# One operation for two expert blocks: silu, multiplication and the copies of the transposed activations in an expert SwiGLU stage

## What is computed

```python
def swiglu(h, wg, wu, wd):
    return (jax.nn.silu(h @ wg) * (h @ wu)) @ wd

def moe_swiglu(h, router, eg, eu, ed):
    ...
    top_v, top_i = lax.top_k(logits, TOP_K)
    ...
    for e in range(N_EXPERTS):
        out = out + combine[:, e:e + 1] * swiglu(t, eg[e], eu[e], ed[e])
```

## Time and profile before

| | |
|---|---|
| median of 3 runs | 1416.88 us (1416.75 to 1418.26) |
| span of the profiled execution | 1415.5 us |
| expert stage in it | from about 450 us to 1403 us |
| PE busy | 1397.5 us, 99% of the span |
| DVE busy | 1147.9 us, 81% |
| ACT busy | 945.4 us, 67% |
| chain that ended last | PE 96%, DVE 3%, ACT 1% |

### The profile page before, as it was taken

The page is one execution under the profiler, slowest core; times in us unless marked ns, Lnnn a source line. Parts: engine busy times, 40 slices in busy tenths (PEclk is TensorE's granted clock), DMA queues, the critical chain, the costliest instruction groups (busy, mean ns, idle before and its releaser), DMA issues.

```text
span 1415.5 us, 18473 instructions
## 1 busy us (share of the span) xinstructions
PE 1397.5 (99%) x6936; PEld 1160.4 (82%) x6937; DVE 1147.9 (81%) x1061; ACT 945.4 (67%) x880; POOL 85.3 (6%) x65
## 2 busy tenths in 40 slices
PE   8999999999999999999999999999999999999997
PEld 6898888887988888888888888888888888888885
DVE  5766645566576989988998998988899899898997
ACT  4645444345646777777777777777777777777775
POOL 2140000001132000000000000000000000000200
PEclk9999999999999999999999999999999999999998
DMA  9434555552444999999999999999999999999992
GB/s 351 162 120 181 208 181 200 183 208 91 148 164 179 361 386 364 387 386 368 383 390 373 375 392 385 361 374 393 370 382 390 373 380 388 389 356 376 421 387 116
DMA packets 63184, 438.20 MB, mean 310 GB/s; under 512 B 7199, under 2 KB 7377, under 8 KB 11906
## 3 DMA queue, kind: packets, MB, share of 16 engines
q1 hardware_dynamic: 58896, 423.20, 78.1%
q0 software_dynamic: 4064, 13.84, 2.5%
q10 hardware_dynamic: 146, 0.07, 0.0%
HBM read 430.79 MB, written 6.29 MB: 309 GB/s over the span
## 4 chain that ended last, share of the span: by engine, by line
PE 96%; DVE 3%; ACT 1%; issue 0%; DMA 0%; DVEq 0%; ACTq 0%
PE ps L1828 50%; PE ps L1852 26%; PE ps L1516 4%; PE ps L1531 3%; PE ps L1619 3%; PE ps L1844 2%; PE ps L1493 2%; PE ps L1888 1%; DVE w_lo L332 1%; PE ps L1608 1%; PE ps L1553 0%; PE ps L1977 0%; PE ps L1563 0%; ACT w_hi L327 0%; PE ps L1474 0%
## 5 line engine op out<-in xcount | busy, mean ns | idle before, releaser
L332 DVE TENSOR_TENSOR w_lo<-raw,w_hi 128x2048 fp32r<-128x2048 f32 x397 | 913.8, 2304 | 173.7 <-ACT w_hi L327 172.0
L327 ACT ACTIVATE w_hi<-raw 128x2048 fp32r<-128x2048 f32 x399 | 764.0, 1915 | 211.6 <-PE ps L1852 109.1
L1828 PE MATMUL ps<-w_hi,xT_hi 128*128 128x512 f32 x1040 | 411.1, 395 | 0.5 <-DVE xT_lo L1196 0.5
L1828 PE MATMUL ps<-w_lo,xT_hi 128*128 128x512 f32 x1040 | 405.5, 390 | 0.0
L1828 PE MATMUL ps<-w_hi,xT_lo 128*128 128x512 f32 x1040 | 404.8, 389 | 0.0
L1828 PEld LDWEIGHTS ps<-w_lo,xT_hi 128*128 128x128 f32 x1040 | 195.2, 188 | 41.6
L1828 PEld LDWEIGHTS ps<-w_hi,xT_hi 128*128 128x128 f32 x1040 | 195.4, 188 | 39.8 <-DVE xT_lo L1196 0.7
L1828 PEld LDWEIGHTS ps<-w_hi,xT_lo 128*128 128x128 f32 x1040 | 195.5, 188 | 38.8
L1852 PE MATMUL ps<-w_hi,aT_hi 128*128 128x512 f32 x524 | 205.9, 393 | 0.0
L1852 PE MATMUL ps<-w_lo,aT_hi 128*128 128x512 f32 x524 | 204.4, 390 | 0.0
L1852 PE MATMUL ps<-w_hi,aT_lo 128*128 128x512 f32 x524 | 204.0, 389 | 0.0
(11 more groups left out here) (307 smaller groups left out, 1112.6 us busy)
## 6 DMA issues: line engine op xcount, KB each, us to landing
raw<-in_stream SPq DMA_DIRECT2D x400, 1024.0 KB, 7.2
outs<-work POOLq DMA_DIRECT2D x7, 512.0 KB, 9.1
gain<-in_gains POOLq DMA_DIRECT2D x4, 512.0 KB, 5.3
h<-in_x SPq DMA_DIRECT2D x2, 512.0 KB, 6.6
raw<-in_stream SPq DMA_DIRECT2D x2, 512.0 KB, 6.1
tokens<-big POOLq DMA_DIRECT2D x2, 512.0 KB, 3.8
out<-work SPq DMA_DIRECT2D x4, 256.0 KB, 2.6
cst<-in_consts SPq DMA_DIRECT2D x1, 581.0 KB, 12.2
```

The costliest lines, as they stand in the source:

```text
L327: nc.scalar.activation(home(n, 0), raw[:, n % RAW, :], ACT.Copy).then_inc(hi_done, 1)
L332: nc.vector.tensor_tensor(home(n, 1), raw[:, n % RAW, :], home(n, 0).bitcast(F32), ALU.subtract).then_inc(lo_done, 1)
L1828: last = nc.tensor.matmul(ps[:, 4 + s, :], (xT_hi, xT_lo)[xp][:, k, x * P:(x + 1) * P], w((n + half), wp, kk * 512, (kk + 1) * 512), start ...
```

## The change

For a pair of expert blocks, silu, multiplication, the high copy and the low part are each one operation over two PSUM banks (128x512 in two pieces of 256 columns) and one semaphore step, where there were two of each. ACT's silu and DVE's multiplication for both blocks stand where those of the second block stood, behind unit m+5. PE has one wait in front of the four transposes of a pair (`pair_T`) and none for the multiplication in the experts' `gate_up`; the exception for the first pair of expert 0 (`next(gu)`) is gone. In the last pair but one of expert 7 all four transposes stand between the two down units; the copies stay single there (`last_aT`), and both come behind unit m+7 on ACT and on DVE. DVE's `last_aT` (not shown) has the two subtractions of the old `ffn_aT`, each behind its wait. The path for crowded experts uses the same functions.

```diff
# ScalarE
+            def pair_silu(g, n, d):
+
+                used(act, n, d)
+                nc.scalar.activation(gate_x[:, :, :], ps[:, 4:6, 0:FB], ACT.Silu).then_inc(fm.silu, 1)
+
+            def pair_aT(g):
+
+                act.wait_ge(fm.aT_ps, g + 1)
+                copy(aT_hi[:, :, :, :].rearrange("p b f q -> p b (f q)"), ps[:, 6:8, 0:FB]).then_inc(fm.aT_hi, 1)
+
+            def last_aT(e, g, n, d):
+
+                act.wait_ge(fm.aT_ps, g + 1)
+                copy(aT_hi[:, 0, :, :], ps[:, 6, 0:FB].rearrange("p (f q) -> p f q", f=2)).then_inc(fm.aT_hi, 1)
+                used(act, n, d)
+                copy(aT_hi[:, 1, :, :], ps[:, 7, 0:FB].rearrange("p (f q) -> p f q", f=2)).then_inc(last_hi, 1)
...
                     hi_unit(act, m + 2, d)
-                    ffn_aT(fm, 1, B, 0)
-                    ffn_aT(fm, 1, B + 1, 1)
+                    pair_aT(g)
                     hi_unit(act, m + 3, d)
-                    ffn_block(fm, 1, B + 2, 0, m + 2, d)
                     hi_unit(act, m + 4, d)
                     if p == 0 and before:
                         y_copy(e - 1, m, d)
                     hi_unit(act, m + 5, d)
-                    ffn_block(fm, 1, B + 3, 1, m + 4, d)
+                    pair_silu(g + 1, m + 4, d)
                     hi_unit(act, m + 6, d)
-                    if ends:
-                        ffn_aT(fm, 1, B + 2, 0)
                     hi_unit(act, m + 7, d)
                     if ends:
-                        ffn_aT(fm, 1, B + 3, 1)
+                        last_aT(e, g + 1, m + 6, d)
...
             def first_pair(e, d):
...
                 hi_unit(act, n + 3, d)
-                ffn_block(fm, 1, B, 0, n + 2, d)
                 hi_unit(act, n + 4, d)
                 hi_unit(act, n + 5, d)
-                ffn_block(fm, 1, B + 1, 1, n + 4, d)
+                pair_silu(e * PAIRS, n + 4, d)
# VectorE
+            def pair_mul(g):
+
+                dve.wait_ge(fm.silu, g + 1)
+                nc.vector.tensor_tensor(act_x[:, :, :], gate_x[:, :, :], ps[:, 4:6, FB:2 * FB], ALU.mult).then_inc(fm.mul, 1)
+
+            def pair_aT(g):
+
+                dve.wait_ge(fm.aT_hi, g + 1)
+                nc.vector.tensor_tensor(aT_lo[:, :, :, :].rearrange("p b f q -> p b (f q)"), ps[:, 6:8, 0:FB],
+                                        aT_hi[:, :, :, :].rearrange("p b f q -> p b (f q)").bitcast(F32),
+                                        ALU.subtract).then_inc(fm.aT_lo, 1)
...
                     lo_unit(dve, m + 2, d)
-                    ffn_aT(fm, 1, B, 0)
-                    ffn_aT(fm, 1, B + 1, 1)
+                    pair_aT(g)
                     lo_unit(dve, m + 3, d)
-                    ffn_block(fm, 1, B + 2, 0, m + 2, d)
                     if p == 1 and follow:
                         dispatch(e + 1, False)
...
                     lo_unit(dve, m + 4, d)
                     lo_unit(dve, m + 5, d)
-                    ffn_block(fm, 1, B + 3, 1, m + 4, d)
+                    pair_mul(g + 1)
...
                     lo_unit(dve, m + 6, d)
-                    if ends:
-                        ffn_aT(fm, 1, B + 2, 0)
                     lo_unit(dve, m + 7, d)
                     if ends:
-                        ffn_aT(fm, 1, B + 3, 1)
+                        last_aT(e, g + 1)
...
             def first_pair(e, d):
...
                 lo_unit(dve, n + 3, d)
-                ffn_block(fm, 1, B, 0, n + 2, d)
                 lo_unit(dve, n + 4, d)
                 lo_unit(dve, n + 5, d)
-                ffn_block(fm, 1, B + 1, 1, n + 4, d)
+                pair_mul(e * PAIRS)
# TensorE
-                        if half == 0 and wait_mul:
-
-                            pe.wait_ge(S.mul, (B - 1) * 2 + (t + 1) if tiles == 2 else B - 1)
+                        if half == 0 and tiles == 2:
+                            pe.wait_ge(S.mul, (B - 1) * 2 + (t + 1))
...
+            def pair_T(g):
+
+                pe.wait_ge(fm.mul, g + 1)
+                for par in range(2):
+                    for f in range(2):
+                        last = nc.tensor.transpose(ps[:, 6 + par, f * P:(f + 1) * P], act_x[:, par, f * P:(f + 1) * P], ident)
+                last.then_inc(fm.aT_ps, 1)
...
                     x = 1 - q if final else q
-                    gu = gate_up(fm, 1, B + 2, 0, m, d, slots_of=e + 1 if final else None, q=x)
-                    if p == 0 and not before:
-                        next(gu)
-                    act_T(fm, 1, B, 0)
-                    act_T(fm, 1, B + 1, 1)
-                    whole(gu)
-                    whole(gate_up(fm, 1, B + 3, 1, m + 2, d, q=x))
+                    pair_T(g)
+                    whole(gate_up(fm, 1, 0, 0, m, d, slots_of=e + 1 if final else None, q=x))
+                    whole(gate_up(fm, 1, 0, 1, m + 2, d, q=x))
...
-                    down(fm, 1, B, 0, m + 4, d, p == 0, False)
+                    down(fm, 1, g, 0, m + 4, d, p == 0, False)
                     if p == PAIRS - 2 and not follow:
-                        act_T(fm, 1, B + 2, 0)
-                    down(fm, 1, B + 1, 1, m + 5, d, False, final)
-                    if p == PAIRS - 2 and not follow:
-                        act_T(fm, 1, B + 3, 1)
+                        pair_T(g + 1)
+                    down(fm, 1, g, 1, m + 5, d, False, final)
```

More of the change, by code:

```diff
@@ L681, in ffn_aT @@
                 act.wait_ge(S.aT_ps, B + 1)
[L682 to L685, removed]
+                copy(aT_hi[:, :, :, :], ps[:, 6 + par, :].rearrange("p (t f q) -> p t f q", t=2, f=2)).then_inc(S.aT_hi, 1)
+            def pair_silu(g, n, d):
[9 more added lines that the diff above has]
+                copy(aT_hi[:, 1, :, :], ps[:, 7, 0:FB].rearrange("p (f q) -> p f q", f=2)).then_inc(last_hi, 1)
             def gathered(k):
@@ L1160, in ffn_aT, with last_aT @@
                 dve.wait_ge(S.aT_hi, B + 1)
[L1161 to L1166, removed]
-                nc.vector.tensor_tensor(dst, src, hi.bitcast(F32), ALU.subtract).then_inc(S.aT_lo, 1)
+                nc.vector.tensor_tensor(aT_lo[:, :, :, :], ps[:, 6 + par, :].rearrange("p (t f q) -> p t f q", t=2, f=2),
+                                        aT_hi[:, :, :, :].bitcast(F32), ALU.subtract).then_inc(S.aT_lo, 1)
+            def pair_mul(g):
[6 more added lines that the diff above has]
+                                        ALU.subtract).then_inc(fm.aT_lo, 1)
+            def last_aT(e, g):
+                dve.wait_ge(fm.aT_hi, g + 1)
+                nc.vector.tensor_tensor(aT_lo[:, 0, :, :], ps[:, 6, 0:FB].rearrange("p (f q) -> p f q", f=2),
+                                        aT_hi[:, 0, :, :].bitcast(F32), ALU.subtract).then_inc(fm.aT_lo, 1)
+                dve.wait_ge(last_hi, e - (N_EXP - 2))
+                nc.vector.tensor_tensor(aT_lo[:, 1, :, :], ps[:, 7, 0:FB].rearrange("p (f q) -> p f q", f=2),
+                                        aT_hi[:, 1, :, :].bitcast(F32), ALU.subtract).then_inc(last_lo, 1)
             def dispatch(e, over):
@@ L1840, in act_T @@
                 for t in range(tiles):
-                    s = t if tiles == 2 else par
                     for f in range(2):
                         c = t * FB + f * P
-                        last = nc.tensor.transpose(ps[:, 6 + par, c:c + P], act_x[:, s, f * P:(f + 1) * P], ident)
+                        last = nc.tensor.transpose(ps[:, 6 + par, c:c + P], act_x[:, t, f * P:(f + 1) * P], ident)
                 last.then_inc(S.aT_ps, 1)
+            def pair_T(g):
[4 more added lines that the diff above has]
+                last.then_inc(fm.aT_ps, 1)
             def down_tile(n, t, a_hi, a_lo, first, final, inner=(0, 1)):
@@ L1919, in expert_end @@
                 unit_ready(n)
-                pe.wait_ge(fm.aT_lo, e * EXP_BLOCKS + EXP_BLOCKS)
+                pe.wait_ge(last_lo, 1)
                 for half in range(2):
@@ L2029, in expert @@
                         pe.wait_ge(y_done, e)
-                    down(fm, 1, B, 0, m + 4, d, p == 0, False)
+                    down(fm, 1, g, 0, m + 4, d, p == 0, False)
                     if p == PAIRS - 2 and not follow:
-                        act_T(fm, 1, B + 2, 0)
-                    down(fm, 1, B + 1, 1, m + 5, d, False, final)
-                    if p == PAIRS - 2 and not follow:
-                        act_T(fm, 1, B + 3, 1)
+                        pair_T(g + 1)
+                    down(fm, 1, g, 1, m + 5, d, False, final)
             def first_pair(e, d):
-                whole(gate_up(fm, 1, e * EXP_BLOCKS, 0, BASE_MOE, d, wait_mul=False, slots_of=e))
-                whole(gate_up(fm, 1, e * EXP_BLOCKS + 1, 1, BASE_MOE + 2, d, wait_mul=False))
+                whole(gate_up(fm, 1, 0, 0, BASE_MOE, d, slots_of=e))
+                whole(gate_up(fm, 1, 0, 1, BASE_MOE + 2, d))
             def alone(e, d, k):
```

24 lines of the change are left out of this document (11 added, 13 removed).

## The result

| | before | after |
|---|---|---|
| median of 5 runs, us | 1418.11 (1416.75 to 1418.66) | 1423.49 (1422.79 to 1425.56) |
| span of the profiled execution, us | 1415.5 | 1420.9 |

The changed kernel is slower: the ratio is 1.0041, with a 95% interval of 1.0030 to 1.0052. That is 5.4 us, in the medians and in the two spans. Forecast were 3.8 us. The kernel before had two further runs by then and its median had risen by 1.2 us. So 1423.5 lies outside the stated range (up to 1422.9) for two reasons: the change costs 1.6 us more than forecast, and the base is 1.2 us higher. On the old base, 1416.9, the 5.4 us would give 1422.3, inside the range by the half of rival (d) that the range took in.

What follows compares the result with a forecast made beforehand. PE was taken as the bound, full in the expert stage, so savings on DVE and ACT gain nothing there. 2.5 + 0.27 + 0.13 - 0.93 + 1.86 = +3.8 us on 1416.9 gave 1420.7 us, range 1418.4 to 1422.9.

Steps and rivals of the forecast that it cites:

- rival (d): TensorE's clock falls in the stalls: 1.9 us per slow stretch, 1422.6 us with one, 1424.5 with two; chance 0.08.
- Part 1: Steady pairs: merges save some 16 us of DVE, 19 of ACT beside a full PE, no gain; slack 0.8 us.
- Part 2: First pair of expert 0: PE stands still before the transposes, waiting for DVE's multiplication; +2.5 us.
- (a): The forecast as summed, +3.8 us, 1420.7 us, own range 1419.6 to 1421.8; chance 0.70.
- Part 3: Expert 0, pairs 0 and 1: longer merged multiplication beside DVE's extra routing work; +0.27 and +0.13 us.
- Part 4: Expert 7, combines: PE's wait in three pairs goes, 0.31 us each; -0.93 us.
- Part 5: The end: PE's down unit of block 12 waits for the low part, now behind `lo_unit(m+7)`; +1.86 us.
- Rival (b): Stalls smaller than worked out; half of those at first pair and end leaves +1.7, 1418.6 us; chance 0.13.
- (e): Merges don't do what they say: a two-bank operation costs two single ones; 1421.2 us; chance 0.02.
- (c): Pairs get shorter at all 55 boundaries by waits taken from PE; at most 6.7 us, 1414.0; chance 0.07.

Runs made afterwards that it cites:

- e7_slack6: Changed kernel with six idle 128x128 operations on VectorE in front of each pair's multiplication; 1433.71 us against 1417.87 for the kernel before, ratio 1.0118.
- e8_fill10: Changed kernel with 10 small unread matmuls on PE in the first pair's stall, before its transposes; 1421.82 us against 1417.87 for the kernel before, ratio 1.0028.
- e8b_fill5: Changed kernel with 5 small unread matmuls on PE at the head of the first pair's stall; 1421.40 us against 1417.46 for the kernel before, ratio 1.0025.
- e2_tail: Changed kernel with block 12's high copy and low part back between units m+6 and m+7; 1421.79 us against 1417.69 for the kernel before, ratio 1.0022.
- e4_both: Changed kernel with expert 0's first pair and the order of the last copies both undone; 1417.90 us against 1417.69 for the kernel before, ratio 0.9999.

## Why the prediction was right or wrong

- **Part 1, steady pairs: right.** No change from pair 3 of expert 0 to pair 3 of expert 7 (4.24 and 4.24). The size of the savings was wrong: 16 us of DVE and 19 of ACT were forecast, 6.5 and 6.6 came. I took the durations of the rows (0.414 twice against 0.683), but a row of DVE overlaps the next instruction by 0.08, so an operation costs 0.33 or 0.60 from start to start, and a merge saves 0.06, not 0.145. Nothing hung on it. The slack was 1.1 on DVE (e7_slack6), not 0.8.
- **Part 2, the first pair: right in mechanism and time, 2.5 forecast, 2.40 measured** (e8_fill10, e8b_fill5). The table load moved behind `hi_unit(n+5)` and DVE decided: its multiplication starts at 462.97, behind its last `lo_unit`, when silu has ended. ACT in order of time, changed kernel:

```profile
460.75 1.28 ACT L688 ACT_TABLE_LOAD   x1
462.04 0.60 ACT L688 ACTIVATE gate_x<-ps 128x512 f32<-128x512 f32 x1
```

  Silu starts right behind the load. The drain that the Trainium skill ("ScalarE: Activation LUTs", What ACT_TABLE_LOAD costs) adds isn't there.
- **The step that failed is the choice of (a) over (d) for this stall: the sum prices part 2 at its idle time and puts the slow matmuls behind it at nothing.** I gave (d) 0.08, on the ground that the engine had been full before. That protects nothing: behind 2.27 us of idle time the granted clock went to 0.50, 1.2 GHz, in the profiled executions of the changed kernel (both) and of e2_tail, by the spans in most others too, and cost 1.57 us (3.97 against 2.40 at pair 1). (d)'s size, 1.9 from the earlier trace rows, was 0.3 too large, and of its two cases the one with a single stall, 5.7 over before, is near the measured 5.4. In the earlier trace rows only the spacing shows the slow stretch: the clock column of the profile has 1.00 from 10 to 16 us.
- **Part 3: 0.27 and 0.13 forecast, 0.23 and 0.04 measured.** Pair 0 in the changed kernel, DVE and PE; the first of three subtractions releases 483.02, 0.88 after the transposes began:

```profile
480.69 6.69 DVE L333 TENSOR_TENSOR w_lo<-raw,w_hi 128x2048 fp32r<-128x2048 f32 x3
...
482.14 0.60 PE L1867 MATMUL ps<-cst,act_x 128*128 128x128 f32 x4
483.02 0.50 PE L1844 MATMUL ps<-w_hi,xT_hi 128*128 128x512 f32 x1 [0.28 <-DVE w_lo L333]
```

- **Part 4: -0.31 per combine forecast; -0.24, -0.21 and, for the last one, -0.28 measured** (in e2_tail the last one with the end is -0.33). The wait is gone as forecast.
- **Part 5: +1.86 forecast, 1.88 measured** (e2_tail against the changed kernel). The rows that answer to the earlier trace rows:

```profile
1400.69 0.39 PE L1875 MATMUL ps<-w_lo,aT_hi 128*128 128x512 f32 x1
1402.72 0.47 PE L1875 MATMUL ps<-w_hi,aT_hi 128*128 128x512 f32 x1 [1.64 <-DVE aT_lo L1185]
...
1397.62 4.62 DVE L333 TENSOR_TENSOR w_lo<-raw,w_hi 128x2048 fp32r<-128x2048 f32 x2
1402.15 0.42 DVE L1185 TENSOR_TENSOR aT_lo<-ps,aT_hi 128x256 fp32r<-128x256 f32 x1
```

`aT_lo` of block 12 now comes behind both `lo_unit`s, at 1402.15, and PE is idle for 1.64 us. Behind this one the clock did not fall, in none of the six profiled executions with a wait of 1.61 to 1.65 us here.
- **Rival (b)** (smaller stalls) and **(e)** (merges without saving) fell by the table and the durations; **(c)** (waits on PE that cost something) fell by e4_both.

The sum with the measured terms is 2.40 + 1.57 + 0.23 + 0.04 - 0.45 + 1.55 (end and last combine together) = 5.3, and 5.34 stands in the table. Without the clock's 1.57 it is 3.77, against a forecast of 3.83. That closeness is in part luck, since parts 2 and 3 came out 0.1 us each below the forecast and part 4 saved 0.15 less.

## What to carry to other kernels

Merging operations that lie beside a full engine gained nothing here, and it made the first and the last block of the pipeline wait for both halves: look at the fill and the drain, not at the steady loop. Price an idle time of the matmul engine of about two us with the slow matmuls that follow it, and split the forecast by that: here they came in three of six traces and by the spans in most executions. Where such an idle time couldn't be avoided, matmuls that nobody reads, for half of it, kept the clock in the trace and in the ten spans of e8b_fill5. Take the cost of an operation from the spacing of its starts, not from its duration.

## What the runs showed of the hardware

- Idle time of PE at the first pair, right behind 11 us of uninterrupted matmuls: 2.27 us and a fall to 1.2 GHz for about 3.4 us (three profiled executions); 2.04, 2.88 and 3.48 us without one (one each); 1.16 us without one. At the end of expert 7: 1.61 to 1.65 us without one (six). What decides is open. In the routing stage the clock fell in five of 13 profiled executions with no idle time over 0.34 us shortly before. The Trainium skill ("TensorE: Matmul & The Clock Gate", Part 1) has the two levels and the return to the lower one after idleness. The levels agree (0.50 and 1.00 in the rows above); the return came behind the stall in three of six.
- What one fall cost at the first pair: 1.57 us, and 1.50 in the second profile of the changed kernel (3.90 against 2.40).
- The operations over two PSUM banks cost as one: 0.680 and 0.683 on DVE, 0.578 and 0.600 on ACT for 512 columns, against 0.683 for 512 columns in one bank.
- The spread of some 3 us between executions of an unchanged kernel goes with the mean granted clock: 1415.4 at 0.998, 1416.0 at 0.997, 1417.4 at 0.996 (mean span, 62 executions of the kernel before).
